# Two kernels of one network block: the second attention's weighted values as three products of high and low parts

## The reference

```python
def _attention(q, k, v):
    ...
    def block(qi):
        s = jnp.einsum('bqhgd,bkhd->bhgqk', qi, k, preferred_element_type=jnp.float32)
        w = jax.nn.softmax(s, axis=-1).astype(v.dtype)
        return jnp.einsum('bhgqk,bkhd->bqhgd', w, v)
```

## Time and profile before

| | |
|---|---|
| median of 3 runs | 2189.32 us (2188.42 to 2189.63) |
| profiled execution | 2189.04 us |
| its span | 2187.2 us |
| PE busy | 2177.7 us |
| DVE busy | 1548.0 us |
| ACT busy | 1063.0 us |
| POOL busy | 120.0 us |
| data moved | 474.97 MB, mean 217 GB/s |

### The profile page before, as it was taken

The page is one execution under the profiler, slowest core; times in us unless marked ns, Lnnn a source line. Parts: engine busy times, 40 slices in busy tenths (PEclk is TensorE's granted clock), DMA queues, the critical chain, the costliest instruction groups (busy, mean ns, idle before and its releaser), DMA issues.

```text
span 2187.2 us, 37567 instructions
## 1 busy us (share of the span) xinstructions
PE 2177.7 (100%) x15900; PEld 2046.9 (94%) x15900; DVE 1548.0 (71%) x1895; ACT 1063.0 (49%) x1398; POOL 120.0 (5%) x111
## 2 busy tenths in 40 slices
PE   9999999999999999999999999999999999999998
PEld 9999999999999889989988988998889999999987
DVE  7899588888889577544554555555768787777776
ACT  5444445544444566444543443444555555444443
POOL 1000000000000400000000000000101111110001
PEclk9999999999999999999999999999999999999999
DMA  8876676687787956656656656656755545688784
GB/s 275 245 241 200 201 251 220 228 280 258 256 277 265 244 188 184 193 192 194 196 195 193 194 193 196 200 192 203 246 174 164 164 144 170 224 272 282 256 279 155
DMA packets 248480, 474.97 MB, mean 217 GB/s; under 512 B 21974, under 2 KB 26448, under 8 KB 247544
## 3 DMA queue, kind: packets, MB, share of 16 engines
q1 hardware_dynamic: 243032, 454.40, 65.5%
q0 software_dynamic: 5280, 18.17, 2.9%
HBM read 468.30 MB, written 5.78 MB: 217 GB/s over the span
## 4 chain that ended last, share of the span: by engine, by line
PE 97%; DMA 1%; DVE 1%; ACT 0%; issue 0%; SPq 0%; DVEq 0%; POOLq 0%; POOL 0%; ACTq 0%
PE ps L917 21%; PE ps L918 21%; PE ps L919 21%; PE ps L910 10%; PE ps L911 10%; PE ps L912 10%; PE ps L835 1%; DMA raw<-in_w_out 1%; PE ps L758 0%; PE ps L708 0%; DMA raw<-in_w_in 0%; PE ps L745 0%; PE ps L824 0%; PE ps L823 0%; PE ps L825 0%
## 5 line engine op out<-in xcount | busy, mean ns | idle before, releaser
L917 PE MATMUL ps<-op0h,whiW 128*128 128x256 f32 x3376 | 937.3, 278 | 0.1
L919 PE MATMUL ps<-op0h,wloW 128*128 128x256 f32 x3376 | 932.8, 276 | 0.0
L918 PE MATMUL ps<-op0l,whiW 128*128 128x256 f32 x3376 | 932.7, 276 | 0.0
L1318 DVE TENSOR_TENSOR wloW<-raw,whiW 128x1024 fp32r<-128x1024 f32 (+1 forms) x503 | 618.3, 1241 | 313.5 <-ACT whiW L964 311.1
L964 ACT ACTIVATE whiW<-raw 128x1024 fp32r<-128x1024 f32 (+1 forms) x504 | 529.3, 1058 | 586.0 <-PE ps L919 471.2
L917 PEld LDWEIGHTS ps<-op0h,whiW 128*128 128x128 f32 x3376 | 633.8, 188 | 2.5 <-issue 1.3
L918 PEld LDWEIGHTS ps<-op0l,whiW 128*128 128x128 f32 x3376 | 633.9, 188 | 0.6
L919 PEld LDWEIGHTS ps<-op0h,wloW 128*128 128x128 f32 x3376 | 633.8, 188 | 0.0
L1318 DVE TENSOR_TENSOR wloT<-raw,whiT 128x1024 fp32r<-128x1024 f32 (+1 forms) x264 | 319.1, 1217 | 237.7 <-ACT whiT L964 236.5
L964 ACT ACTIVATE whiT<-raw 128x1024 fp32r<-128x1024 f32 (+1 forms) x264 | 274.0, 1046 | 286.2 <-PE ps L912 228.9
L910 PE MATMUL ps<-whiT,op1h 128*128 128x512 f32 x640 | 249.3, 390 | 0.3 <-DVE wloT L1318 0.3
(11 more groups left out here) (314 smaller groups left out, 2106.8 us busy)
## 6 DMA issues: line engine op xcount, KB each, us to landing
raw<-in_w_in SPq DMA_DIRECT2D x256, 512.0 KB, 4.3
raw<-in_w_up SPq DMA_DIRECT2D x128, 512.0 KB, 3.8
raw<-in_w_down SPq DMA_DIRECT2D x128, 512.0 KB, 4.1
raw<-in_w_ada SPq DMA_DIRECT2D x96, 512.0 KB, 4.6
raw<-in_w_gate SPq DMA_DIRECT2D x96, 512.0 KB, 5.1
raw<-in_w_out SPq DMA_DIRECT2D x64, 512.0 KB, 5.3
raw<-in_w_branch SPq DMA_DIRECT2D x48, 512.0 KB, 5.1
raw<-in_w_proj_a SPq DMA_DIRECT2D x24, 512.0 KB, 5.0
```

What stands on the lines that cost most here:

```text
L917: pe.matmul(o, wh, xh[:, ka, :], start=first and m % 2 == 0, stop=False, skip_group_check=True)
L918: pe.matmul(o, wh, xl[:, ka, :], start=False, stop=False, skip_group_check=True)
L919: mm = pe.matmul(o, wl, xh[:, ka, :], start=False, stop=last, skip_group_check=True)
L1318: v.tensor_tensor(wlo[job.mode][q % NSPL][:, :, 0:job.n], x, h.bitcast(F32), ALU.subtract).then_inc(s_lo, 1)
```

## The change

Three things are edited. The weighted values of the second attention (`values2` on TensorE) are made as three products of high and low parts. For that there are new parts of work: `prob_high` and `prob_low` of each head's exponentials at q+6 (ScalarE) and q+7 (VectorE), and `split_v` for the values of the context (`vc`) and of the input (`vx`). TensorE's `values2` moves from q+7 to q+8. Several waits make the buffers free that the new parts share with others. The tables `rct` and `rst` are kept for one head instead of four and read by broadcast in `rotate`, which now has one buffer `rot[2]` for both halves of the rows. The gate buffers `ga` and `gb` lie in another order. The five output semaphores become one.

```diff
-    rc = np.tile(np.stack([co, co], 2).reshape(256, 128), (1, 4))
-    rs = np.tile(np.stack([-si, si], 2).reshape(256, 128), (1, 4))
-    rc = rc.reshape(2, 128, 512).transpose(1, 0, 2).reshape(128, 1024)
-    rs = rs.reshape(2, 128, 512).transpose(1, 0, 2).reshape(128, 1024)
+    rc = np.stack([co, co], 2).reshape(2, 128, 128).transpose(1, 0, 2).reshape(128, 256)
+    rs = np.stack([-si, si], 2).reshape(2, 128, 128).transpose(1, 0, 2).reshape(128, 256)
...
+        for name, q in (("vc", of["k"].end + 3), ("vx", of["vx"].end + 2)):
+            for tt in range(2):
+                side(act_at, q + tt, "split_v", name, tt)
+                side(dve_at, q + 1 + tt, "split_v", name, tt)
...
                 side(act_at, q + 5, "softmax2_exp", h)
-                side(pe_at, q + 7, "values2", h)
+                side(pe_at, q + 8, "values2", h)
                 side(dve_at, q + 6, "softmax2_sum", h)
+                side(act_at, q + 6, "prob_high", h)
+                side(dve_at, q + 7, "prob_low", h)
             side(dve_at, q + 8, "softmax2_share", i)
...
-        rct = bg("rct", [128, 2, 512], 44)
-        rst = bg("rst", [128, 2, 512], 48)
+        rct = bg("rct", [128, 2, 128], 44)
+        rst = bg("rst", [128, 2, 128], 45)
+        vxh, vxl, vcl = bg("vxh", [128, 2, 512], 46, F32R), bg("vxl", [128, 2, 512], 40, F32R), bg("vcl", [128, 2, 512], 4, F32R)
+        vch = [bg("vch0", [128, 512], 50, F32R), bg("vch1", [128, 512], 67, F32R)]
+        probh = [[bg(f"probh{r}", [128, 4, 256], 8 + r, F32R) for r in rows] for rows in ((8, 8, 8, 8, 4, 4), (12, 12, 0, 0, 0, 0))]
+        probl = [at(f"probl{e}", [128, 4, 256], tmp_at + 4096 * e, F32R) for e in range(2)]
...
-        ga = [bg(f"ga{i}", [128, 4, 256], 56 + 4 * i) for i in range(2)]
-        gb = [bg(f"gb{i}", [128, 4, 256], 64 + 4 * i) for i in range(2)]
+        ga = [bg(f"ga{i}", [128, 4, 256], 56 + 8 * i) for i in range(2)]
+        gb = [bg(f"gb{i}", [128, 4, 256], 60 + 8 * i) for i in range(2)]
...
             def values2(h):
                 e, kv = h % 2, h // 3
                 if h == 0:
-                    pe.wait_ge(s_pair[of["vx"].pair], of["vx"].after)
-                pe.wait_ge(s_exp2, h + 1)
+                    pe.wait_ge(s_vl, 4)
+                pe.wait_ge(s_pl, h + 1)
+                o, ph, pl = bank[4][:, 256 * e:256 * e + 256], probh[e][h // 2], probl[e]
                 for st in range(4):
-                    vv = vx if st < 2 else vc
-                    mm = pe.matmul(bank[4][:, 256 * e:256 * e + 256], vv[:, st % 2, 128 * kv:128 * kv + 128], keyed[e][:, st, :],
-                                   start=st == 0, stop=st == 3)
+                    d = slice(128 * kv, 128 * kv + 128)
+                    vh = vxh[:, st, d] if st < 2 else vch[st - 2][:, d]
+                    vl = (vxl, vcl)[st // 2][:, st % 2, d]
+                    pe.matmul(o, vh, ph[:, st, :], start=st == 0, stop=False)
+                    pe.matmul(o, vh, pl[:, st, :], start=False, stop=False)
+                    mm = pe.matmul(o, vl, ph[:, st, :], start=False, stop=st == 3)
                 mm.then_inc(s_av2, 1)
...
+            def prob_high(h):
+                e, i = h % 2, h // 2
+                act.wait_ge(s_exp2, h + 1)
+                if i == 4:
+                    act.wait_ge(s_share2, 4)
+                elif i == 2:
+                    act.wait_ge(s_share2, 2)
+                if h >= 2:
+                    act.wait_ge(s_av2, h - 1)
+                act.activation(probh[e][i][:, :, :], keyed[e][:, :, :], ACT.Copy).then_inc(s_ph, 1)
...
             def ep_silu(job, b0, b1):
                 if job.arg == 0:
                     act.wait_ge(s_xw, 16)
+                elif job.arg == 8:
+                    act.wait_ge(s_av2, 7)
+                elif job.arg == 12:
+                    act.wait_ge(s_av2, 4)
...
-                    if which == "b" and c == 1:
+                    if c == 1:
+                        act.wait_ge(s_av2, 12)
                         act.wait_ge(s_atv, 12)
...
             def rotate(s, tt):
-                t1, t2 = rot[tt], rot[2 + tt]
+                t1, t2 = rot[tt], rot[2]
...
+                v.wait_ge(s_rot, 2 * s + tt)
...
+            def prob_low(h):
+                e, p = h % 2, keyed[h % 2]
+                v.wait_ge(s_ph, h + 1)
+                v.wait_ge(s_sum2, h + 1)
+                v.tensor_tensor(probl[e][:, :, :], p[:, :, :], probh[e][h // 2][:, :, :].bitcast(F32), ALU.subtract).then_inc(s_pl, 1)
+
+            def split_v(name, tt):
+                x, h, l = ((vc[:, tt, :], vch[tt][:, :], vcl[:, tt, :]), (vx[:, tt, :], vxh[:, tt, :], vxl[:, tt, :]))[name == "vx"]
+                v.wait_ge(s_vh, tt + 1 + 2 * (name == "vx"))
+                v.tensor_tensor(l, x, h.bitcast(F32), ALU.subtract).then_inc(s_vl, 1)
+
             def values2(h):
...
-                v.wait_ge(s_av2, h + 1)
+                v.wait_ge(s_av2, h - e + 2)
```

More of the change, by code:

```diff
@@ L396, in program @@
         peak, total = at("peak", [128, 2, 256], tmp_at + 10240), bg("total", [128, 2, 256], 69)
-        rot = [bg(f"rot{i}", [128, 512], 61 + 2 * i) for i in range(4)]
+        rot = [bg(f"rot{i}", [128, 512], 61 + 2 * i) for i in range(3)]
         mgh, mgl = bg("mgh", [128, 16, 256], 24, F32R), bg("mgl", [128, 16, 256], 40, F32R)
-        ga = [bg(f"ga{i}", [128, 4, 256], 56 + 4 * i) for i in range(2)]
-        gb = [bg(f"gb{i}", [128, 4, 256], 64 + 4 * i) for i in range(2)]
+        ga = [bg(f"ga{i}", [128, 4, 256], 56 + 8 * i) for i in range(2)]
+        gb = [bg(f"gb{i}", [128, 4, 256], 60 + 8 * i) for i in range(2)]
         gbc = bg("gbc", [128, 2048], 0)
@@ L466, in program @@
         s_sig = sem("z_sigmoid")
+        s_ph, s_pl, s_vh, s_vl = sem("prob_high"), sem("prob_low"), sem("values_high"), sem("values_low")
         s_sc2, s_scr2, s_max2, s_peak2, s_less2, s_exp2, s_sum2, s_total2, s_share2, s_av2, s_atv, s_ahi, s_att = (
@@ L475, in program @@
             sem("final_gain"), sem("x3_rows"), sem("x3_square"), sem("x3_gained"), sem("out_rows0"), sem("out_rows1"))
-        s_out = [sem(f"out{i}") for i in range(5)]
+        s_out = sem("out")
         norms = [("x0", 0), ("x0", 1), ("ctx", 0), ("mixed", 0), ("mixed", 1), ("x1", 0), ("x1", 1), ("kc", 0), ("kc", 1),
@@ L537, in _ @@
                     sp.wait_ge(s_fin, (1, 2, 3, 0, 4)[i])
-                sp.dma_start(rows[:, tt, c0:c1], X2[:, tt, c0:c1]).then_inc(s_out[i], 16)
-            for i in range(5):
-                sp.wait_ge(s_out[i], 16)
+                sp.dma_start(rows[:, tt, c0:c1], X2[:, tt, c0:c1]).then_inc(s_out, 16)
+            sp.wait_ge(s_out, 80)
         landed, fills = {}, [0] * NRAW
@@ L1087, in softmax2_exp @@
                 act.activation(p[:, :, :], p[:, :, :], ACT.Exp, scale=ATT_SCALE).then_inc(s_exp2, 1)
+            def prob_high(h):
[9 more added lines that the diff above has]
+            def split_v(name, tt):
+                x, h = ((vc[:, tt, :], vch[tt][:, :]), (vx[:, tt, :], vxh[:, tt, :]))[name == "vx"]
+                if name == "vc":
+                    act.wait_ge(s_pair[of["vc"].pair], of["vc"].after)
+                else:
+                    act.wait_ge(s_pair[of["vx"].pair], of["vx"].after)
+                act.activation(h, x, ACT.Copy).then_inc(s_vh, 1)
             def values2(h):
@@ L1107, in _ @@
                      "turn1": turn1, "values1": values1, "scale_qk": scale_qk, "turn_qk": turn_qk, "scores2": scores2, "softmax2_exp": softmax2_exp,
-                     "values2": values2, "fourier_t": fourier_t, "fourier_d": fourier_d, "split_kc": split_kc}
+                     "values2": values2, "prob_high": prob_high, "split_v": split_v, "fourier_t": fourier_t, "fourier_d": fourier_d, "split_kc": split_kc}
             def ep_copy(job, b0, b1):
@@ L1587, in rotate @@
             def rotate(s, tt):
-                t1, t2 = rot[tt], rot[2 + tt]
-                sv, dv, rv = (x.rearrange("p (a h f) -> p a h f", h=2, f=32) for x in (t1[:, :], t2[:, :], rst[:, tt, :]))
+                t1, t2 = rot[tt], rot[2]
+                sv, dv = (x[:, :].rearrange("p (n a h f) -> p n a h f", a=2, h=2, f=32) for x in (t1, t2))
+                rv = rst[:, tt, :].rearrange("p (a h f) -> p a h f", h=2, f=32).unsqueeze(1).broadcast_to([128, 4, 2, 2, 32])
                 if s == 1 and tt == 0:
@@ L1592, in rotate @@
                 v.wait_ge(s_qks, 2 * s + tt - 1)
-                v.tensor_tensor(dv[:, :, 0, :], sv[:, :, 1, :], rv[:, :, 0, :], ALU.mult)
-                v.tensor_tensor(dv[:, :, 1, :], sv[:, :, 0, :], rv[:, :, 1, :], ALU.mult).then_inc(own.sem, own.up())
+                v.wait_ge(s_rot, 2 * s + tt)
+                v.tensor_tensor(dv[:, :, :, 0, :], sv[:, :, :, 1, :], rv[:, :, :, 0, :], ALU.mult)
+                v.tensor_tensor(dv[:, :, :, 1, :], sv[:, :, :, 0, :], rv[:, :, :, 1, :], ALU.mult).then_inc(own.sem, own.up())
                 v.wait_ge(own.sem, own.n)
```

(5 more changed lines are left out.)

1 line of the change is left out of this document (added).

## The result

The changed kernel takes 2213.46 us (median of 4, 2211.24 to 2215.59) beside 2188.88 us for the kernel before in the same comparison: ratio 1.0112, 95% interval 1.0099 to 1.0124, 24.6 us more. Its profiled execution took 2212.92 us with a span of 2211.1 us, 23.9 us more than the one of before. The prediction was 2205 us with a range to 2211: the direction is right, a third of the loss is missing, and the time lies outside the range.

A forecast was written before the change was run, and what follows sets the result against it. The prediction took TensorE, busy without gaps, to bound the kernel: 2189.0 us before + 19.3 of waits - 3.7 saved by shorter products + 0.6 for restarts = 2205.2, so 2205 us, range 2195 to 2211.

The forecast's parts named there:

- What bounds the kernel: Whole span: TensorE busy for all but 10 us; only work taken from it pays, any wait is paid in full.
- Multiplications: `values2` on TensorE: 24 instructions in 2.88 us replace 16 costing 3.50 us; saves 0.62 us a pair, 3.7 in all.
- The wait: TensorE before `values2`: six waits for the first `prob_low`, held until all-reduce start + 4.22 us in most pairs; 19.3 us.
- the port does not hold `prob_low`: Rival at the low parts: each ends 1.22 us after its turn; waits 10.4 us, total 2196 us; chance 0.14.
- the low part starts only when the all-reduce has ended: Rival at the low parts: five waits 1.13 us longer each, total 2211 us; chance 0.07.
- What is late next: VectorE's list behind the low parts: 2.44 us later, but TensorE is later too; no further wait at weight chunks.
- at nothing: `split_v`, `rotate`, gate waits, output semaphore: priced zero; for `split_v`, VectorE 24 and ScalarE 29 us to spare, 1590 to 1625.
- TensorE's clock falls in a wait: Rival behind the waits: half rate for a stretch, about 2.1 us each; once 2207, after three 2211; chance 0.15.
- the sum: Forecast total for the changed kernel: 2189.0 + 19.3 - 3.7 + 0.6 = 2205.2 us, 0.7% slower.
- allowance of 0.1 us for each restart: TensorE restarting after each of six waits: 0.6 us in all, an allowance that no row shows.
- falls behind three waits: Upper case of the clock rival: TensorE's clock falls after three waits, total 2211 us; the rival's chance 0.15.
- The other side: Rival at `values2`: waits hidden because sums and low parts come earlier relative to TensorE; 2185.3 us; chance 0.08.

The follow-up runs named there:

- e9: Changed kernel with the pair's chain one position earlier, prob_low right behind its sum and the all-reduce held until both low parts are done: 2187.95 us.
- e5: Changed kernel with a pair's chain from softmax2_less to the low parts one position earlier, the values left in place: 2190.09 us, ratio 1.0005.
- e7: Changed kernel with prob_low one position earlier (q+6), right behind the sum of its head: 2197.90 us, ratio 1.0043.
- e3: Changed kernel with GpSimd's all-reduce of the totals held back until both low parts of the pair are done: 2203.53 us, ratio 1.0068.
- e1: Kernel before with only one-head tables read by broadcast, shared rotation buffer, reordered gate buffers with earlier wait, one output semaphore: 2188.88 us, ratio 1.0000.
- e2: Changed kernel with TensorE multiplying the identity with itself before the wait for each pair's first low part: 2204.51 us, ratio 1.0072.
- e12: e9 with the values' VectorE multiplication at q+8 in pairs 0 to 4; in pair 5 share at q+9, values at q+10: 2185.97 us, ratio 0.9984.
- e13: e9 with one wait put in: in pair 5 TensorE's values wait for the end of the totals' all-reduce: 2191.36 us, ratio 1.0010.
- e10: e9 with softmax2_share one position earlier (q+7): 2190.63 us, ratio 1.0009.
- e4: Changed kernel with the values one position later on TensorE (q+9), VectorE's and ScalarE's values parts one later too: 2197.10 us, ratio 1.0040.

## Why the prediction was right and where it was wrong

**What bounds the kernel** held: TensorE, with every wait paid in full.

**Multiplications.** Foreseen 0.62 us a pair, 3.7 us in all. In e9 the stretch from the first product of the values to the second matmul behind them is 0.57 us shorter than before, 3.4 us in all. Right.

**The wait.** Six waits foreseen at 19.3 us, measured 18.6; the first low part was foreseen at the all-reduce's start + 4.22 us, and in pair 0 it is there at 1670.52 + 3.27 = 1673.79, which is the start at 1669.56 + 4.23. That this figure is the same in pair after pair was luck in part: e5 and e7 record the all-reduce with 3.23 us where no subtraction is ahead of it, and the 0.9 us more of the earlier trace rows are there because each time a weight half starts just before it. e3 shows that it is the all-reduce: with it out of the way 10.6 us are left, against 10.4 of the rival "the port does not hold `prob_low`". That rival is refuted as a whole, though its 10.4 us are more than half of the wait. So is the rival in which the low part starts only when the all-reduce has ended: the first low part of pair 0 ended 0.10 us after the all-reduce's recorded end, not 1.22.
The Trainium skill (SBUF — State Buffer, on the shared port pair) has it that whichever of the two starts first has the pair for its whole instruction and that the other is blocked. The trace agrees that one of the two is held, in either direction (e7); which of them started first it can't show there, and by the recorded ends the hold is over about 1.1 us before the all-reduce is.

**What is late next** and **at nothing** held in the changed kernel: no wait at any weight chunk in the stretch, and the rest of the change alone costs nothing (e1). The 24 and 29 us to spare, though, are those of the whole 68 us of the earlier trace rows and not of 1590 to 1625.

**Where it failed: the step "TensorE's clock falls in a wait".** It was given 0.15, on the ground that only pair 5's wait is long, and was priced at 2.1 us once; the sum itself put it at nothing. The clock fell in five of the six waits, those of 2.52 to 5.33 us; only the 2.03 us of pair 3 left it at its upper level. Price by e2: 2213.46 - 2204.51 = 9.0 us. With it the sum closes: 18.6 + 9.0 - 3.4 = 24.2 us, measured 24.6. The trace of the changed kernel alone gives the same account within a microsecond: 18.6 us of waits, 8.1 us more than forecast for the products behind them, 3.4 us saved, 23.3 in all, where its span is 23.9 us longer. The sum's allowance of 0.1 us for each restart is what pair 3 shows, 2.98 us for 2.88. The error was in the reasoning as much as in the number: the trace of before has no wait to learn from, and I took "cannot show it" for "unlikely". Even the case of falls behind three waits, 2211, was too mild: five times its 2.1 us would have given 2205.2 + 10.5 = 2216. The 2.1 us were too much for four of the five falls (1.3 to 1.5 us each) and about right for pair 5 (2.2). They came from the earlier trace rows, nine instructions, which are not nine products but four and a half; they run at half the later rate, yet the profile's granted clock stands at 1.00 there, so that row could not show the level.

**The other side** (waits hidden) happened in no kernel without moving the work. It took three edits of order: the chain a position earlier, the low part ahead of the all-reduce, the share and the values' epilogue at the places where the look-ahead had room (e12).

**What stays open.** In e13 the 24 products behind the wait take 4.36 - 2.88 = 1.5 us longer, where 1.6 was expected; the medians give 3.4 - 3.2 + 1.0 = 1.2 us and can't be trusted to a microsecond, as said there. What decides whether a wait lowers the clock is open. Its length alone does not: waits of 1.92 (e10), 2.18 (e7) and 2.47 us (e5) were followed by a fall, waits of 2.03 (pair 3 of the changed kernel), 2.07 (e4) and 2.79 us (e7) were not. Open too is whether the wait would shrink if no weight half stood ahead of the all-reduce, whose end would then come some 0.9 us earlier; no run tries it.

## What to carry to other kernels

On a kernel whose bound is TensorE without gaps, price a new wait as its length plus what the stretch at half clock behind it costs: here 18.6 us of waits cost some 27 us. Waits from 1.92 us on were followed by a fall of the clock here, though not all of them. Before adding a VectorE instruction with two SBUF inputs to a path, look for a GpSimd reduction that starts at the same moment, and have the reduction wait for the instruction; right behind the sum, let go by the same event as the reduction, was not enough (e7). A table with, for every chunk, when its operand is ready and when TensorE comes for it shows where side work has room; the average busy share doesn't.

## What the runs showed of the hardware

- In the changed kernel TensorE's granted clock fell to 0.50 for a stretch with each wait of 2.52 us and more, products starting every 0.21 us instead of 0.12; with that of 2.03 us it stayed at 1.00. In the other runs a wait of 1.92 us was followed by a fall (e10) and one of 2.79 us was not (e7). Matmuls on the identity in the waiting time kept it at 1.00 (e2), which gains 9.0 us by the medians without any useful work.
The Trainium skill (TensorE: Matmul & The Clock Gate, the HAM clock gate) says that idling throttles the array; the trace agrees, and for waits shorter than I had thought.
- A VectorE subtraction with two SBUF inputs that GpSimd's all-reduce holds is recorded with up to 3.31 us instead of 1.22 and ends about 0.1 us after the all-reduce's record. One with an input in PSUM is not held: the two `ep_pb` products (line 1857) run during the all-reduce of pair 5 and are recorded, as all eight of that line, with 0.67 to 0.69 us each.
- The all-reduce is held as well: it is recorded with 3.23 to 3.24 us where nothing is ahead of it, with 4.13 where a weight half started 0.18 us before, and with 4.33 in the pairs of e7 where the low part got its way.
- Two instructions let go by the same semaphore event had recorded starts within 0.02 us of each other (e7); which of them was held differed from pair to pair, and over 2 us of VectorE's time hung on it.
